# Differential attention in a hybrid encoder block: alternating score pieces, a running minimum, one reciprocal per row, and the lambda product on GpSimd

## What is computed

```python
def blk(qp, q1b, q2b):
    mask = _chunk_mask(qp, kpos)
    bias = jnp.where(mask[None], -slopes[:, None, None] * dist[None], NEG)
    s1 = jnp.einsum('bhqd,bhkd->bhqk', q1b, k1).astype(f32) * scale + bias
    s2 = jnp.einsum('bhqd,bhkd->bhqk', q2b, k2).astype(f32) * scale + bias
    a = jax.nn.softmax(s1, axis=-1) - lam * jax.nn.softmax(s2, axis=-1)
    return jnp.einsum('bhqk,bhkv->bhqv', a.astype(v.dtype), v)
```

## Time and profile before

| what | value |
| --- | --- |
| median of three runs | 2601.21 us (2600.6 to 2601.32) |
| span of the profiled execution | 2600.7 us (no other time of that execution is given) |
| differential attention | about 432 to 797 us of the span |
| in 432 to 795 us: PE busy | 348.8 of 363 us |
| DVE busy | 318.9 us |
| ACT busy | 260.1 us |
| POOL busy | 77.3 us |

### The profile page before, as it was taken

One profiled execution on the slowest core, in us unless ns is written; L12 is line 12 of the kernel. 1 busy time (PEld: TensorE's weight loads), 2 busy tenths in 40 slices (PEclk: granted clock), 3 DMA queues, 4 the chain that ended last, 5 costly groups with the idle time before them and its releaser, 6 DMA issues.

```text
span 2600.7 us, 35372 instructions
## 1 busy us (share of the span) xinstructions
PE 2540.5 (98%) x12220; PEld 2114.9 (81%) x12220; DVE 1614.7 (62%) x3499; ACT 1212.5 (47%) x2183; POOL 332.0 (13%) x368
## 2 busy tenths in 40 slices
PE   8999999999999999999999999999999999999997
PEld 7998888777667999977877888888888888888886
DVE  6123306998995776654458677876757465564765
ACT  6112314777764555554544333533335353443554
POOL 1110002222221222210000000000000001111143
PEclk9999999999999999999999999999999999999999
DMA  7334458553332111135677767657655365776787
GB/s 232 122 106 125 126 163 253 143 135 87 93 131 90 36 31 45 41 110 158 194 247 220 221 200 237 218 182 216 190 161 179 110 221 108 171 167 162 203 162 137
DMA packets 329436, 398.59 MB, mean 153 GB/s; under 512 B 21408, under 2 KB 235664, under 8 KB 320944
## 3 DMA queue, kind: packets, MB, share of 16 engines
q1 hardware_dynamic: 311696, 364.41, 44.7%
q0 software_dynamic: 17568, 31.99, 8.4%
HBM read 239.86 MB, written 156.48 MB: 152 GB/s over the span
## 4 chain that ended last, share of the span: by engine, by line
PE 62%; DVE 3%; DMA 1%; ACT 1%; issue 1%; SPq 0%; POOL 0%; DVEq 0%; ACTq 0%; POOLq 0%
PE ff_ps_x L3262 26%; PE ff_ps_m L3262 13%; PE ff_ps_z L3262 6%; PE ml_ps_s L2139 6%; PE ff_ps_m L1695 4%; PE ml_ps_o L2168 4%; PE ml_ps_t L2152 2%; DMA ml_v_raw<-scr_yT 1%; DMA ff_pieces<-scr_acc 0%; PE ff_ps_r L2699 0%; PE mo_ps_t L2716 0%; SPq L2326 0%; DVE ff_pieces L2429 0%; DVE ff_pieces L2620 0%; DVE ff_pieces L2616 0%
## 5 line engine op out<-in xcount | busy, mean ns | idle before, releaser
L3262 PE MATMUL ff_ps_x<-ff_mv_hi_p,ff_st_hi_p 128*128 128x512 f32 x764 | 297.8, 390 | 0.5 <-ACT ff_u L3002 0.5
L3262 PE MATMUL ff_ps_x<-ff_mv_hi_p,ff_st_lo_p 128*128 128x512 f32 x764 | 297.3, 389 | 0.0
L3262 PE MATMUL ff_ps_x<-ff_mv_lo_p,ff_st_hi_p 128*128 128x512 f32 x764 | 297.2, 389 | 0.0
L2139 PE MATMUL ml_ps_s<-wide,ml_qs 128*128 128x416 f32 (+14 forms) x880 | 195.6, 356 | 3.7 <-PEq L137 2.7
L3108 DVE TENSOR_TENSOR ff_st_lo_p<-ff_ps_m,ff_st_hi_p 128x512 fp32r<-128x512 f32 x190 | 130.8, 689 | 103.4 <-ACT ff_st_hi_p L2985 103.4
L2952 POOL DMA_DIRECT2D scr_acc<-ff_pieces x64 | 55.5, 872 | 1015.3 <-DVE ff_pieces L3132 946.9
L3002 ACT ACTIVATE ff_u<-ff_ps_x 128x512 f32<-128x512 f32 x128 | 76.6, 598 | 215.0 <-PE ff_ps_x L3262 215.0
L3262 PEld LDWEIGHTS ff_ps_x<-ff_mv_hi_p,ff_st_hi_p 128*128 128x128 f32 x764 | 143.4, 188 | 32.4 <-issue 2.0
L3262 PEld LDWEIGHTS ff_ps_x<-ff_mv_hi_p,ff_st_lo_p 128*128 128x128 f32 x764 | 143.4, 188 | 29.9
L3262 PEld LDWEIGHTS ff_ps_x<-ff_mv_lo_p,ff_st_hi_p 128*128 128x128 f32 x764 | 143.4, 188 | 29.6
L2139 PEld LDWEIGHTS ml_ps_s<-wide,ml_qs 128*128 128x128 f32 x880 | 152.0, 191 | 16.3 <-issue 2.9
(11 more groups left out here) (318 smaller groups left out, 6349.7 us busy)
## 6 DMA issues: line engine op xcount, KB each, us to landing
st_raw<-in_w_ff SPq DMA_DIRECT2D x64, 512.0 KB, 6.2
scr_hid<-ff_pieces SPq DMA_DIRECT2D x128, 256.0 KB, 2.7
st_raw<-scr_hid SPq DMA_DIRECT2D x64, 512.0 KB, 5.4
ring<-in_w_ff SPq DMA_DIRECT2D x28, 1024.0 KB, 7.7
scr_t<-ring SPq DMA_DIRECT2D x24, 1024.0 KB, 5.8
ring<-scr_t SPq DMA_DIRECT2D x21, 1024.0 KB, 8.1
scr_acc<-ff_pieces POOLq DMA_DIRECT2D x64, 256.0 KB, 4.1
ring<-scr_u SPq DMA_DIRECT2D x13, 1024.0 KB, 8.4
```

The source lines that it names most:

```text
L2139: m = pe.matmul(ps_s[n % NSB][:, 0:w], q, k, start=j == 0, stop=j == len(pairs) - 1)
L3262: m = pe.matmul(bank[:, :], w[kind][:, k], a[kind][:, k], start=start and k == 0 and i == 0, stop=stop and k == KH - 1 and i == 2, skip_gr ...
```

## The change

1. The pieces of a row alternate between the maps (first map's piece, second map's piece, and so on) where before all of the first came ahead of all of the second.
2. Each read of a piece takes the minimum of the negated scores and starts from the minimum of the piece before in the same map; the row keeps negated, scaled scores and `exp` uses a scale of -1 with the last piece's minimum as its bias. The operation for the row maximum (L1538) is gone; `exp` waits for the read of the map's last piece.
3. One reciprocal over both sums takes the place of two. It stands in `scale`, and waits for the exponentials of both maps. GpSimd makes the product with minus lambda, ahead of its multiplication of the row, in each `scale`.
4. The small tiles have eight places where there were two, and the second map of rows 0 and 1 has a place of its own (`second_small`).
5. `scale` and `end` are placed by cost: after 2 row widths + 600 and 3 row widths + 1200, in units of a column plus 230 for a piece. What is due is put in ahead of a row's first piece by what that piece overwrites.

The core of the diff:

```diff
-        chunks = [(i, c, k0, n) for i in range(NT) for c in range(COMPS) for k0, n in row_chunks(i)]
+        chunks = [(i, c, k0, n) for i in range(NT) for k0, n in row_chunks(i) for c in range(COMPS)]
...
+        def second_before(i):
+            return i - NT if i < SMALL else i - 2 - SMALL if i < SMALL + 2 else i - 2
...
+                    if k0 == 0:
+                        now, later = due(i - NRB if c == 0 else second_before(i))
+                        steps += now
                     steps += [("chunk", 0, n)]
-                    later = [(left - 1, step) for left, step in later]
-                    steps += [step for left, step in later if left <= 0]
-                    later = [(left, step) for left, step in later if left > 0]
+                    later = [(left - cost(("chunk", 0, n)), step) for left, step in later]
+                    ready = [step for left, step in later if left <= 0]
+                    later = [(left - sum(cost(step) for step in ready), step) for left, step in later if left > 0]
+                    steps += ready
                     if k0 + w == META + P * (i + 1):
-                        steps += [step for _, step in later if step[2] - NT * step[1] < i]
-                        later = [(left, step) for left, step in later if step[2] - NT * step[1] >= i]
                         later.append((1, ("exp", 0, i, c)))
-                        if c == 0:
-                            later.append((SCALE_AFTER, ("scale", 0, i)))
                         if c == COMPS - 1:
-                            later.append((END_AFTER, ("end", 0, i)))
+                            width = META + P * (i + 1)
+                            for kind, left in (("scale", 2 * width + SCALE_AFTER), ("end", 3 * width + SCALE_AFTER + END_AFTER)):
+                                later.append((max([left] + [at for at, step in later if step[0] == kind]), (kind, 0, i)))
...
             def scaled(h, i, u, **at):
                 hold(pool, inv_ready, NT * h + i + 1)
-                pool.tensor_scalar(row(i, u), row(i, u), inv[:, i % 2, 0:1], 1.0, ALU.mult, ALU.mult).then_inc(first_scaled, 1)
+                pool.tensor_scalar(inv2[:, i % NRB:i % NRB + 1], inv[:, i % NRB, 1:2], lam[:, 3:4], 1.0, ALU.mult, ALU.mult).then_inc(inv2_ready, 1)
+                pool.tensor_scalar(row(i, u), row(i, u), inv[:, i % NRB, 0:1], 1.0, ALU.mult, ALU.mult).then_inc(first_scaled, 1)
...
+                if nth:
+                    dve.wait_ge(scores_read, NCH * h + n - COMPS + 1)
                 hold(dve, scores_ready, NCH * h + n + 1)
                 dve.tensor_tensor_reduce(out=comp_row(i, c, u)[:, k0:k0 + w], in0=ps_s[n % NSB][:, 0:w],
-                                         in1=bias[u][:, b0:b0 + w], scale=1.0, scalar=LOWEST,
-                                         op0=ALU.add, op1=ALU.max,
-                                         accum_out=mx[:, i % 2, c, nth:nth + 1]).then_inc(scores_read, 1)
-                if k0 + w == META + P * (i + 1):
-                    dve.wait_ge(scores_read, NCH * h + n + 1)
-                    dve.tensor_scalar(nmax_all[:, 0:nth + 1], mx[:, i % 2, c, 0:nth + 1], -scale, None, ALU.mult, ALU.min,
-                                      accum_out=nmax[:, i % 2, c:c + 1]).then_inc(max_ready, 1)
+                                         in1=bias[u][:, b0:b0 + w], scale=-scale,
+                                         scalar=mx[:, i % NRB, c, nth - 1:nth] if nth else -LOWEST,
+                                         op0=ALU.add, op1=ALU.min,
+                                         accum_out=mx[:, i % NRB, c, nth:nth + 1]).then_inc(scores_read, 1)
...
             def invert(h, i, u, **at):
-                dve.wait_ge(exp_ready, NT * COMPS * h + COMPS * i + 1)
-                dve.reciprocal(inv[:, i % 2, 0:1], total[:, i % 2, 0:1]).then_inc(inv_ready, 1)
...
+                dve.wait_ge(exp_ready, NT * COMPS * h + COMPS * (i + 1))
+                dve.reciprocal(inv[:, i % NRB], total[:, i % NRB]).then_inc(inv_ready, 1)
```

64 lines of the change are left out of this document (36 added, 28 removed).

## The result

| | median | lowest to highest | runs |
| --- | --- | --- | --- |
| before | 2601.27 us | 2600.6 to 2603.75 | 4 |
| changed | 2639.55 us | 2634.09 to 2640.83 | 4 |

The changed kernel takes 1.0142 times as long, with a 95% interval of 1.0129 to 1.0156. That is 38 us slower, where 16 us were forecast, and outside the range of 2603 to 2629 us. The sign was right and the size was not.

The account below looks back on a forecast made before the run. TensorE was taken to set the pace, 80.5 us of work in a head's 86.47 us. Inside of heads +6.4, boundaries +6.0, first head -2.0, tail +1.0, clock +5 us on 2600.7 gave 2617 us; range 2603 to 2629 us.

Parts of the forecast that it names:

- the size of VectorE's relief: VectorE in a head: loses 13.6 us of 78.5 (row maximum, one reciprocal in two, lambda product), busy near 65 us after.
- the boundary chain: Between heads: exponentials, reciprocal, GpSimd's operations and `end` make TensorE wait 5.4 us where waits were 3.4; +2.0 us, three times.
- mid-head: First turn of group 2: TensorE waits 2.4 to 2.6 us for the `end` of row 11, once a head, four times.
- the first head: First head, run without older products: of some 2.6 us of waits in its first rows, 2 us are given back.
- the tail: After the last head: 8.9 us from the last piece to the turn, before 6.9; less 0.9 us, so +1.0 us.
- the inside of a head: Waits for a bank behind VectorE inside a head: 1.3 us a head given back, 0.4 us added in row 15.
- 0.4 us there: Row 15 of each head: reads delayed by the `end` of row 13 cost TensorE 0.4 us, upper end 1 us.
- I count one for each: Clock: one fall per boundary, about 1.3 us each, +4 us; mid-head falls in 4 of 10, 1 us taken; +5 together.
- The rival C: Every long wait drops the clock, seven falls at 1.7 us, and start values cost 80 ns: 2628 us; chance 0.20.
- The start value: Each read's start value from memory: priced at nothing, upper end 4.5 us a head on VectorE.
- The wait between reads: Each read on VectorE waits for the read two before it: already met, since another read lies between; no cost.
- rival D: Fewer VectorE instructions are what counts: 13.6 us less a head takes away all waits behind VectorE, 2575 us; chance 0.02.

Follow-up runs that it names:

- The first experiment: The changed kernel with spare transposes on TensorE ahead of the first turn of group 2 (20) and group 3 (40): 2622.08 us, 1.0081 of before.
- the best version: The changed kernel with earlier scales and ends of rows 11, 14, 15, 8 products held back instead of 6, 14 and 26 spare transposes: 2607.67 us.

## Why the prediction was wrong in size

The first experiment splits the miss. Without the clock the changed kernel stands at 2622.1 us, where the sum ahead of the clock was 2600.7 + 11.4 = 2612.1. So 10 us of the 22.5 are waits and 12.5 us are clock (11 if the clock is taken as 16 us). Both kernels keep two stretches of 3.4 us in this comparison, the kernel before at 778 and 802 us, the other at 823 and 1342 us.

- **Right: what bounds the kernel.** TensorE's own work and the waits ahead of turns set the time. VectorE was busy 73.22 us in a head where it was 78.49, and the head became longer.
- **Wrong, with no share in the miss: the size of VectorE's relief.** The 13.6 us a head were added up from durations, and the signs had VectorE busy near 65 us. It was 73.22. The kernel with constant start values has 70.33, so 2.9 us of the gap are the start value. The rest is that short operations overlap their neighbours: in the kernel before, a reciprocal of 0.16 us starts at 597.52 and the next read at 597.60. Of the 13.6 us of durations only 78.46 - 70.33 = 8.1 us were VectorE's time.
- **Right: the boundary chain.** 5.4 us forecast, 5.6 from start to start (the last score matmul starts at 615.8 us and takes 0.18). The reciprocal starts 6.3 us after the last piece of row 15 (610.09 to 616.43), where the forecast had 5.95; from there on each link is within 0.1 us.
- **Right in kind, 0.45 us short: mid-head.** 2.4 to 2.6 forecast, 2.95 measured.
- **Too kind, by 1.4 and 0.7 us: the first head and the tail.** From the first score matmul to the first turn of the first head pass 27.3 us (before 27.9), where I gave back 2. In the tail the last score matmul is done at 802.92, when the product behind it starts, and the turn comes at 812.51, 9.6 us later; the forecast had 8.9.
- **Wrong: the inside of a head.** I gave back 1.3 us of bank waits and added 0.4 us in row 15. Of the 92.56 us period without clock loss, 80.5 are work, 5.6 and 2.95 the two turns; 3.5 us are left, where the forecast had 2.6 - 1.3 + 0.4 = 1.7. The largest part of that is one wait of 1.27 us (605.42), behind the `end` of row 13. That `end` must stand ahead of row 15's first piece in `da_second`, whose place it frees, and with alternation that piece comes second in its row instead of sixth. The mis-sized term is "0.4 us there", with an upper end of 1 us. The other part of the 1.8 us is in the 1.3 us that I gave back and that didn't all come; no run takes it apart further. The alternating pieces alone make the same wait, of 1.19 us. Together 0.2 us at three boundaries, and 0.45 and 1.8 us in four heads: 9.6 us. With the first head and the tail that is 11.7 us. The trace of the first experiment has just that: 368.3 us from the first score matmul to the tail's turn (431.86 to 800.12), where the forecast adds 11.4 us to the 345.1 of before. The split by medians, which takes in all behind that turn too, has 10.
- **Wrong, and the largest: the clock.** The step that failed is "I count one for each, about 1.3 us since part of the low stretch falls into the wait", and the 1 us taken for mid-head. A boundary's stretch lasted 6.8 us, not the 3.4 us of the tail in the earlier trace rows, and about 4 us of it lay on work behind the wait: 2 us, three times. In mid-head it fell four times in four, not in 4 of 10, and 3.0 us of each lay on work, in the last head 6.1: 1.5 us three times and 3 us once, where I took 1 us in all. And the tail and the end of the stage, for which the sum has no further clock loss, went from two stretches of 3.4 us to two of 6.8. Together 17.5 us (16 by the ratios), not 5. The rival C had seven falls at 1.7 us and came to 2628 us; it too took the length of a fall from the one fall in the earlier trace rows.
- **The start value.** I took nothing, and in the changed order that is about right (0 to 0.6 us a head), though the price is real: 55 to 56 ns a read. C's 80 ns was near it, its 1 us a head was not.
- **The wait between reads.** "The wait is met by then, since another read lies between" held: alternating reads of 416 columns follow each other in 0.57 us (800.28 and 800.85 in VectorE's timeline of the changed kernel), that is the 0.51 of before and the start value's 0.06. That the same wait without alternation costs 0.26 us a read, more than the row maxima that it saves, was not in my sum and shows what alternation is for here.
- **The rules of the Trainium skill.** By the rule named with rival D (the Trainium skill, VectorE: DVE Perf Modes, Rules for kernel authors) fewer VectorE instructions should have paid. The trace has 208 of them a head in place of 305 and a period 9.1 us longer. The rule in TensorE: Matmul & The Clock Gate of the Trainium skill, HAM oscillation, that each wait across an idle stretch leaves cold work behind it, agrees with the changed kernel's trace at every wait of 2.95 us and more. It fails at some waits of this length in the other runs: that of 3.62 us at 611.87 in the kernel with earlier scales brought no fall, nor did the tail's wait of 3.02 us in the kernel with the start value from memory.

Still open: what sets whether a wait of some 3 us brings a stretch at half clock at all, and whether the stretch lasts 3.4 or 6.8 us (776 and 810 us differ between two kernels with the same waits to 0.2 us), and 2.3 us a head between the best version (88.80) and before (86.47). The two turns' waits of some 3.0 and 1.6 us are there in place of 1.95, which is 2.65 us, so they can be all of it.

## What to carry to other kernels

An engine that is nearly full is not the bound by that: take work off it only where another engine waits for it, and count what the new order puts behind the last piece before you count what it saves. When a change makes waits on TensorE near the length of one that brought a fall (here 2.7 us and more), price each with the work behind it at half clock, for more than the length of the one stretch seen so far; spare work in the wait, cut to the wait's length, shows the clock's share in one run. An accumulator carried from one operation to the next is cheap only if another operation lies between the two.
